# Feed-forward output projections: the high weight tile streams both parts of the operand in one 512-column pass

## The reference

```python
T, D_MODEL, D_FF = 256, 1024, 2816

def swiglu(x, w_in, w_out):
    a, b = jnp.split(x @ w_in, 2, axis=-1)
    return (jax.nn.silu(a) * b) @ w_out
...
x = x + 0.5 * swiglu(rmsnorm(x, ffn1_norm[l]), w_ffn1_in[l], w_ffn1_out[l])
```

## Time and profile before

| | |
|---|---|
| median of 3 runs | 2360.81 us (2360.24 to 2362.17) |
| the profiled execution | 2363.54 us |
| its span, first to last instruction | 2361.6 us |
| TensorE busy | 2337.7 us, 99% |
| VectorE busy | 1637.2 us, 69% |
| ScalarE busy | 1278.4 us, 54% |
| GpSimd busy | 354.1 us, 15% |
| mean granted TensorE clock | 0.998 |

### The profile page before, as it was taken

The page is one execution under the profiler, slowest core; times in us unless marked ns, Lnnn a source line. Parts: engine busy times, 40 slices in busy tenths (PEclk is TensorE's granted clock), DMA queues, the critical chain, the costliest instruction groups (busy, mean ns, idle before and its releaser), DMA issues.

```text
span 2361.6 us, 50717 instructions
## 1 busy us (share of the span) xinstructions
PE 2337.7 (99%) x21742; PEld 2278.6 (96%) x21742; DVE 1637.2 (69%) x2260; ACT 1278.4 (54%) x1831; POOL 354.1 (15%) x303
## 2 busy tenths in 40 slices
PE   9999999999999999999999999999999999999998
PEld 8999999999999999999999999989999999989998
DVE  6765787976667657878666766776766666776763
ACT  6654655654455456565555544645544554636554
POOL 4011020300200210203003002431002002431001
PEclk9999999999999999999999999999999999999999
DMA  6555433555555544335555655422545555422553
GB/s 252 196 197 180 178 125 133 186 198 189 195 189 196 197 178 179 124 130 191 200 186 189 223 179 197 157 91 89 213 175 198 204 179 197 168 80 91 216 179 124
DMA packets 57679, 410.20 MB, mean 174 GB/s; under 512 B 6384, under 2 KB 6640, under 8 KB 8688
## 3 DMA queue, kind: packets, MB, share of 16 engines
q1 hardware_dynamic: 56592, 402.15, 47.3%
q10 hardware_dynamic: 864, 4.82, 0.5%
HBM read 405.89 MB, written 1.05 MB: 172 GB/s over the span
## 4 chain that ended last, share of the span: by engine, by line
PE 83%; DVE 7%; ACT 4%; issue 4%; POOL 1%; DMA 1%; SPq 0%; DVEq 0%; ACTq 0%; POOLq 0%
PE bank L556 83%; DVE sb_wlo L512 3%; DVE area L1837 1%; ACT sb_whi L504 1%; DMA sb_raw<-stream 1%; PE bank L2185 1%; ACT area L1557 0%; DVE area L1820 0%; DVE area L1786 0%; DVE area L646 0%; POOL sb_x_ssq L699 0%; ACT area L1623 0%; ACT area L1578 0%; DVE area L1894 0%; ACT area L1581 0%
## 5 line engine op out<-in xcount | busy, mean ns | idle before, releaser
L556 PE MATMUL bank<-area,sb_whi 128*128 128x256 f32 x11752 | 2022.7, 278 | 4.5 <-ACT area L780 1.8
L556 PEld LDWEIGHTS bank<-area,sb_whi 128*128 128x128 f32 x11752 | 1772.8, 188 | 15.4 <-issue 4.2
L556 PE MATMUL bank<-area,sb_wlo 128*128 128x256 f32 x5876 | 1610.8, 278 | 5.3 <-DVE sb_wlo L512 5.0
L504 ACT ACTIVATE sb_whi<-sb_raw 128x1024 fp32r<-128x1024 f32 x762 | 792.8, 1055 | 604.4 <-PE bank L556 590.8
L556 PEld LDWEIGHTS bank<-area,sb_wlo 128*128 128x128 f32 x5876 | 1095.9, 188 | 8.0 <-DVE sb_wlo L512 7.9
L512 DVE TENSOR_TENSOR sb_wlo<-sb_raw,sb_whi 128x1024 fp32r<-128x1024 f32 x762 | 955.1, 1265 | 165.5 <-ACT sb_whi L504 163.7
L646 DVE TENSOR_TENSOR area<-bank,sb_x_diag 128x512 f32<-128x512 f32 x244 | 167.2, 686 | 70.3 <-PE bank L556 49.8
L979 DVE TENSOR_TENSOR area<-area,area 128x256 f32<-128x256 f32 x176 | 76.3, 434 | 189.6 <-ACT area L930 188.8
L556 PE MATMUL bank<-area,area 64*64 64x64 f32 (+5 forms) x2864 | 149.6, 249 | 0.1
L556 PEld LDWEIGHTS bank<-area,area 64*64 64x64 f32 (+3 forms) x2864 | 127.4, 139 | 19.1 <-ACT area L1605 5.3
L691 POOL TENSOR_TENSOR sb_x_ssq<-sb_x 128x256 f32<-128x256 f32 x9 | 12.0, 1331 | 853.1 <-DVE sb_x L1018 842.9
(11 more groups left out here) (269 smaller groups left out, 1179.4 us busy)
## 6 DMA issues: line engine op xcount, KB each, us to landing
sb_raw<-stream SPq DMA_DIRECT2D x379, 1024.0 KB, 4.8
sb_raw<-stream SPq DMA_DIRECT2D x4, 512.0 KB, 7.3
area<-lora ACTq DMA_DIRECT2D x2, 768.0 KB, 6.7
area<-c ACTq DMA_DIRECT2D x1, 1504.0 KB, 7.2
sb_x<-x SPq DMA_DIRECT2D x4, 256.0 KB, 5.3
area<-mem ACTq DMA_DIRECT2D x1, 1024.0 KB, 9.6
out<-sb_x SPq DMA_DIRECT2D x4, 256.0 KB, 2.9
area<-m ACTq DMA_DIRECT2D x1, 512.0 KB, 5.5
```

The lines of the kernel that those rows point to most:

```text
L504: e.activation(k.hi[k.slot[p]], raw_piece(k, p), ACT.Copy).then_inc(*k.done("weights_hi", p))
L556: return e.matmul(out, lhsT, rhs, start=start, stop=stop, skip_group_check=True, tile_position=at)
```

## The change

The high and low parts of a hidden tile come to lie side by side (`m.both`, 22 x 2 x 256), so that a hidden tile is 512 columns in a row. A new function `gemm_both` takes the place of `gemm` in the output phase. For each weight tile, one pass streams the 512 columns over the high weights and writes both halves of the PSUM bank, and a second pass streams the high part over the low weights and adds to the first half. In the first product of a stage, the last two tiles keep three passes, since their hidden tiles come last. VectorE adds the second half of the bank to `k.x` and then the first half, two dependent instructions where there was one.

```diff
+def gemm_both(e, k, b, m, says, first=None):
+    for i in range(NF):
+        p, wh, wl, begins, ends = take(k)
+        if begins:
+            e.wait_ge(*k.when("weights_hi", p))
+        if first is not None and i >= NF - 2:
+            e.wait_ge(*k.when("hidden_hi", first, i))
+            mm(e, b[:, 0:T], wh, m.hh[:, i, :], False, False)
+            e.wait_ge(*k.when("hidden_lo", first, i))
+            mm(e, b[:, T:2 * T], wh, m.hl[:, i, :], False, i == NF - 1)
+        else:
+            if first is not None:
+                e.wait_ge(*k.when("hidden_hi", first, i))
+                e.wait_ge(*k.when("hidden_lo", first, i))
+            mm(e, b[:, 0:2 * T], wh, flat(m.both[:, i]), i == 0, i == NF - 1)
+        if begins:
+            e.wait_ge(*k.when("weights_lo", p))
+        end = mm(e, b[:, 0:T], wl, m.hh[:, i, :], False, i == NF - 1)
+        if i == NF - 1:
+            end.then_inc(*k.done("product", *says, also=("used", p) if ends else None))
+        elif ends:
+            end.then_inc(*k.done("used", p))
...
 def ffn_tiles(k):
     m = State()
-    m.hh, m.hl = area(k, 0, NF, T, dt=F32R), area(k, NF * T, NF, T, dt=F32R)
+    m.both = area(k, 0, NF, 2, T, dt=F32R)
+    m.hh, m.hl = m.both[:, :, 0, :], m.both[:, :, 1, :]
...
     for j in range(NX):
         mark = ("x", s, j)
-        b = main_bank(e, k, *mark)
-        if j == 0:
-            gemm(e, k, b[:, 0:T], m.hidden, mark, ("hidden_hi", s), ("hidden_lo", s))
-        else:
-            gemm(e, k, b[:, 0:T], m.hidden, mark)
+        gemm_both(e, k, main_bank(e, k, *mark), m, mark, s if j == 0 else None)
...
         b = bank_at(k, "x", s, j)
         e.wait_ge(*k.when("product", "x", s, j))
+        e.scalar_tensor_tensor(k.x[:, j, :], b[:, T:2 * T], 0.5, k.x[:, j, :], ALU.mult, ALU.add).then_inc(
+            *k.done("x_begun", s, j))
+        e.wait_ge(*k.when("x_begun", s, j))
         e.scalar_tensor_tensor(k.x[:, j, :], b[:, 0:T], 0.5, k.x[:, j, :], ALU.mult, ALU.add).then_inc(
             *k.done("x", s, j))
```

## The result

The changed kernel takes 2381.84 us (median, 2381.45 to 2382.13) against 2360.52 us, a ratio of 1.0091 (95% interval 1.0079 to 1.0103): 21.3 us slower, where +10.5 was forecast, and above the range of 2352 to 2378. The sign was right. The size was not.

The account below looks back on a forecast made before the run. TensorE's issue of passes was taken as the bound in the output phase. Against the median, 2360.81 + 10.5 (9.3 for the passes, 1.2 for the ends) = 2371.3 us, 0.44% slower; range 2352 to 2378 us.

Parts of the forecast that it names:

- What bounds the kernel: Output phase: TensorE's issue of passes sets the end, at 340 ns a tile, 113.3 ns a pass; other engines have room.
- The wide pass: Output phase: the added 512-column pass takes 233.3 ns, replacing two 256-column passes of 226.7 ns together, on 1392 tiles.
- Kept: one pass of 256 columns over the low weights: Output phase: the remaining narrow low-weight pass stays at 113.3 ns, making a tile 346.7 ns, +9.3 us over 1392 tiles.
- rival 1: Output phase, also called first rival: low pass slows too, to 117.4 or 120.0 ns; 2376.9 or 2380.6 us; chance 0.23.
- The bounds: Output phase: wide pass between 213.3 and 240.0 ns; upper narrow pace 120.0 ns; whole between 2352 and 2378 us.
- Moved and added: Output phase: earlier waits for low hidden parts cost 0; 64 VectorE additions are hidden except at ends, +1.2 us.
- the ends: Behind a stage's last product and at kernel end: the added VectorE additions are uncovered, +1.2 us together (0.9 to 2).
- waits that should grow: TensorE waits for L780 by tenths of a microsecond; last norm and A1f2 to B0f1 by 0.46 us each.
- A loss per column at the good pace: Rival 2, output phase: wide pass 226.7 ns, tile stays at 340, only the ends left, 2362.0 us; chance 0.24.
- A loss once per pass: Rival 3, output phase: wide pass 220.0 ns, tile 333.3, -9.3 us, 2352.7 us with the ends; chance 0.19.

Follow-up runs that it names:

- e2: Changed kernel with the low weights also streamed over all 512 columns, adding the low x low part (extra work); 2524.26 us.
- e3: Changed kernel with all weight slots on a multiple of 512 bytes (LINE 0 in place of 64); 2439.5 us.
- e12: Changed kernel with two narrow passes for each wide one, except one wide pass at every product's eleventh tile; 2379.63 us against 2359.48, ratio 1.0085.
- e14: Changed kernel with narrow passes, except one wide pass per stage at the first product's fourth tile; 2379.2 us in one run, beside 2361.69 before.
- e1: Changed kernel with its wide pass cut into two 256-column passes, layout and both additions kept; 2361.69 us against 2358.87, ratio 1.001.
- e11: Changed kernel taking four tiles at a time where possible, four wide passes then four narrow; 2371.98 us.
- e5: Changed kernel taking two tiles at a time: wide, wide, narrow, narrow; 2369.04 us against 2358.90, ratio 1.0041.
- e4: Changed kernel with weight slots 128 bytes below a multiple of 512 (LINE 128 in place of 64); 2423.01 us.
- e10: Changed kernel with two narrow passes for each wide one and each stage's hidden tiles moved up by 64 bytes more than the last's; 2372.86 us.
- e6: Changed kernel with the narrow low-weight pass writing the second half of the bank, not the first; 2379.36 us.
- e9: Changed kernel, wide passes kept, with the hidden tiles of stage n (0 to 7) moved up by 64 n bytes; 2382.99 us.

## Why the prediction was wrong

**What bounds the kernel: right.** TensorE's issue of passes sets the time in the output phase, VectorE waits for TensorE before each addition, and no engine took its place.

**The wide pass: right within a nanosecond on the mean, and that is luck.** 233.3 was taken. In the changed kernel the wide pass has 233.7 on the mean. But the row it came from does not carry over: e2 has the same operands at 228.9, the first wide pass of a stage takes 226, and e3 has the mixers' passes at 226.7 after a move of the weights by 64 bytes.

**The step that failed is "Kept: one pass of 256 columns over the low weights".** It was left at 113.3 ns. It goes to 119.5: the tile is 353.2, not 346.7, so the change costs 13.2 ns x 1392 = 18.4 us there, not 9.3. The prediction had this as its first rival, all passes at the slow pace, priced at 350.7 ns a tile or, with the narrow pass at 120.0, at 353.3 ns and 2380.6 us, within 2 us of the result. But the rival got the smaller part of the chance. Its argument against, that the pace had been 113.3 right after the fifth slot's piece, was made on a train of three equal passes. e12 and e14 show that a single wide pass is enough to end that pace for every pass behind it, through the end of the phase.

The prediction says that it can't read from the rows what puts a stretch at one pace or the other. The trace of the kernel before shows more than it read. In the stage B0f1, TensorE waits once for low weights, for 0.43 us. The tile that starts at 1302.40 us, ahead of the wait, takes 0.34 us, the one at 1304.14, behind it, 0.35, and the slow pace is there until 1417 us:

```profile
1302.40 0.39 PE L556 MATMUL bank<-area,sb_whi 128*128 128x256 f32 x2
...
1302.74 0.39 PE L556 MATMUL bank<-area,sb_whi 128*128 128x256 f32 x2
1303.56 0.39 PE L556 MATMUL bank<-area,sb_wlo 128*128 128x256 f32 x1 [0.43 <-DVE sb_wlo L512]
...
1304.14 0.40 PE L556 MATMUL bank<-area,sb_whi 128*128 128x256 f32 x2
...
1304.49 0.40 PE L556 MATMUL bank<-area,sb_whi 128*128 128x256 f32 x2
...
L556 PE MATMUL bank<-area,sb_wlo x148: 278/280/287, 1312.0 to 1363.9; 128*128 128x256 f32 x148
L556 PE MATMUL bank<-area,sb_wlo x156: 278/281/283, 1362.9 to 1417.7; 128*128 128x256 f32 x156
L556 PE MATMUL bank<-area,sb_wlo x148: 275/277/277, 1423.8 to 1473.8; 128*128 128x256 f32 x148
```

The last three lines are stretches of the same stage: 353 ns (51.9 us / 147), 354 (54.8 / 155) and 340 (50.0 / 147). All their passes are narrow, and the slots lie where they lie in the stages at 340. So the good pace is a state that can be lost without any wide pass too. A piece in the fifth slot at 1355 us left the slow pace as it was; the next one, at 1417 us, stands where it turned into the good one. That a fifth-slot piece sets the good pace again was thus never sure, and that was the ground on which the narrow pass was left at 113.3.

**The bounds.** The upper ends for a wide and a narrow pass together would have been 240 + 120 = 360 ns. The range stopped at 2378, short of the 2380.6 that rival 1 named, and the measured time lies above both. The 117.4 ns of the earlier trace rows is 117.8 over longer stretches, a matter of rounding.

**Moved and added: right in kind, small in size.** Additions come in twos, 0.46 us apart, hidden but at the ends:

```profile
657.18 0.42 DVE L1042 SCALAR_TENSOR_TENSOR sb_x<-bank,sb_x 128x256 f32<-128x256 f32 x1 [3.28 <-PE bank L556]
657.64 0.42 DVE L1045 SCALAR_TENSOR_TENSOR sb_x<-bank,sb_x 128x256 f32<-128x256 f32 x1
```

e1 has all that is not the wide pass at 2.8 us (0 to 4.7), where 1.2 was forecast, 0.9 to 2 its range; the interval takes in both. The two terms, 18.4 and 2.8, are 21.2 of the 21.3 us; with 0 to 4.7 us on the second, so close a fit is partly luck. The change of state in B0f1 is a term of its own that can go either way: between 1372.1 and 1416.9 us the changed kernel has 133 tiles, at 340 ns, where the kernel before had 128, at 353, some 2 us gained that no term of the forecast had. One small term was not foreseen: the slow pace goes on into the next stage's opening, seven passes in 0.82 us for 0.79, and its eighth waits for x(7), as forecast: 0.86 us from 657.80 to 658.66. Of the waits that should grow, the one in the last norm did (0.5 to 1.0 us in all); the one between A1f2 and B0f1 grew by 0.1 us and not by 0.46; and those for high parts (L780, now L807) went from 1.8 us down to 0.5.

**The rivals.** A loss per column at the good pace (340 ns) was seen for one pass a stage, the first wide one, at 0.22 us. No place, order or rhythm tried kept it. A loss once per pass (220.0 ns) was seen in no steady stretch: the quickest rhythm of wide passes over hidden tiles has 228.9, and the mixers' best 226.7. The section "Wait — 56ns, not 53.3ns?" of the page "TensorE: Matmul & The Clock Gate" of the Trainium skill gives 215.7 ns for back-to-back warm matmuls of 512 columns; no steady stretch of wide fp32r passes here has it.

**What stays open.** Why a wide pass or a wait ends the state, why one fifth-slot piece sets it again and another does not, why no rhythm with a wide pass holds it, and why e11 is slower than e5, no run explains. The rows show how the loss stays inside the phase: in the next stage's pairs, from 663.4 to 699.9 us, 107 tiles take 36.5 us, 341 ns each, after its first fifth-slot piece. That the paces of narrow passes hang on the addresses that are read is shown by e3, e4 and e10, and that the half written last doesn't matter, by e6; whether the length of a write matters, no run tells. Whether the weight load or the stream loses the time was not separated, since each pass brings its own load.

No version beats the kernel before. Beside a narrow pass at 113.3, the wide pass would have to take under 226.7 ns, and no steady stretch had that.

## What to carry to other kernels

Before two passes are merged into one, look whether the pace of the train is a property of each pass or of the train: here 1392 merged passes cost 18.4 us, and 8 of them nearly as much (17.5 us, one execution beside one). Look in the trace that you have for equal passes at equal places that run at two paces: that is the sign of a state. Price what stays at the pace that the new rhythm will have, not at the one it has now. A cheap probe is one odd pass in a train of equal ones, and the distance between starts behind it. And look where the operands lie first: at two of the four distances the same merge would have saved time per tile.

## What the runs showed of the hardware

- Back-to-back fp32r passes of 256 columns, each with its own weight load, had four steady paces here, at a mean granted clock of 0.998 or 0.999 of 2.4 GHz: 113.3, 117.8, 118.7 and 120.0 ns a pass (340, 353.3, 356 and 360 ns for three). The distance between the addresses of stream and weights decides, with a period of 256 bytes: 64 or 192 bytes allow 340, 128 gives 356, 0 gives 360 (e3, e4, e10); 353.3 was seen at the distances that allow 340. So what a pass takes hangs here on both addresses together.
- At a distance that allows 340, the train can also stay at 353.3. One pass of 512 columns put it there, and the 172 narrow tiles behind it did not get it out (e14). In the kernel before, a wait of TensorE of 0.43 us stands where the pace went from 340 to 353, and it stayed there for 113 us.
- With wide and narrow passes in turn, the tile is 351 to 353 ns at all eight places (e9), below the 356 and 360 ns of three narrow passes at the same places in four of them (e10).
- Wide passes with the weights streaming take 233.3 ns with the stream 64 bytes below a multiple of 512 and 226.7 ns with it on one (the earlier trace rows and e3).
